# Three Strassen tile pairs per gate chunk, and Strassen tiles in the output projection of a decoder layer, on one core

## The reference, cut to what matters

```
h   = RMSNorm(x)
[u_pool | q | f | i | g | gate_a | gate_b] = h @ W_in       # 2048 x 9216
y_a = W_a( pooled differences of u_pool, mixed in 4 groups )
y_b = W_b( gated linear recurrence of q, f, i, g in 8 heads )
merged = sigmoid(gate_a) * y_a + sigmoid(gate_b) * y_b
x  += merged @ W_out                                        # 2048 x 2048
x  += W_down( silu(conv(u)_gate) * conv(u)_val ),  u = RMSNorm(x) @ W_up
x  += sigmoid(RMSNorm(x) @ W_pg) * (p @ W_ple)
out = RMSNorm(x)
```

## Time and profile before

| What | Value |
|---|---|
| median of three runs | 1432.59 us (1432.58 to 1432.82) |
| the profiled execution | 1433.02 us |
| its span, first to last instruction | 1431.2 us |
| PE busy | 1420.7 us, 99% |
| DVE busy | 1033.4 us, 72% |
| ACT busy | 774.3 us, 54% |
| POOL busy | 171.5 us, 12% |
| share of PE in the chain that ended last | 97% |
| granted TensorE clock, mean | 0.999 |
| transfers | 273.47 MB, 191 GB/s over the span |

### The profile page before, as it was taken

The page is one execution under the profiler, slowest core; times in us unless marked ns, Lnnn a source line. Parts: engine busy times, 40 slices in busy tenths (PEclk is TensorE's granted clock), DMA queues, the critical chain, the costliest instruction groups (busy, mean ns, idle before and its releaser), DMA issues.

```text
span 1431.2 us, 19783 instructions
## 1 busy us (share of the span) xinstructions
PE 1420.7 (99%) x7094; PEld 1207.4 (84%) x7094; DVE 1033.4 (72%) x1284; ACT 774.3 (54%) x937; POOL 171.5 (12%) x115
## 2 busy tenths in 40 slices
PE   9999999999999999999999999999999999999997
PEld 7888888888888888888888888888888888888886
DVE  7676777867577765566777777777777888887755
ACT  7555655545454544455555555555555555555644
POOL 0044144100000000000111101111011110000000
PEclk9999999999999999999999999999999999999999
DMA  9655555455665665466656566565665555566663
GB/s 323 199 176 162 161 170 169 147 189 193 193 204 177 220 236 189 156 206 185 190 176 205 177 191 194 173 204 181 192 193 180 202 197 194 174 197 215 231 200 121
DMA packets 190876, 273.47 MB, mean 191 GB/s; under 512 B 11744, under 2 KB 103136, under 8 KB 190688
## 3 DMA queue, kind: packets, MB, share of 16 engines
q1 hardware_dynamic: 190384, 272.30, 59.4%
q10 hardware_dynamic: 432, 0.37, 0.1%
HBM read 270.53 MB, written 2.10 MB: 190 GB/s over the span
## 4 chain that ended last, share of the span: by engine, by line
PE 97%; DVE 1%; issue 0%; DMA 0%; ACT 0%; SPq 0%; ACTq 0%; POOLq 0%; POOL 0%; DVEq 0%
PE aux L839 11%; PE main L839 11%; PE main L661 10%; PE main L663 10%; PE main L662 10%; PE aux L848 6%; PE main L848 6%; PE main L719 5%; PE main L720 5%; PE main L721 5%; PE aux L719 3%; PE aux L720 3%; PE aux L721 3%; PE aux L662 2%; PE aux L661 2%; PE aux L663 2%
## 5 line engine op out<-in xcount | busy, mean ns | idle before, releaser
L1421 DVE TENSOR_TENSOR w_lo<-raw,w_hi 128x1024 fp32r<-128x1024 f32 (+1 forms) x484 | 596.8, 1244 | 337.8 <-ACT w_hi L1119 337.4
L1119 ACT ACTIVATE w_hi<-raw 128x1024 fp32r<-128x1024 f32 (+1 forms) x484 | 508.6, 1052 | 517.3 <-PE main L663 158.4
L661 PE MATMUL main<-w_hi,xT 128*128 128x512 f32 x510 | 201.4, 395 | 0.5 <-DVE w_lo L1883 0.3
L662 PE MATMUL main<-w_lo,xT 128*128 128x512 f32 x510 | 198.6, 389 | 0.0
L663 PE MATMUL main<-w_hi,xT 128*128 128x512 f32 x510 | 198.5, 389 | 0.0
L839 PE MATMUL aux<-xT,w_hi 128*128 128x512 f32 x704 | 169.8, 391 | 0.0
L839 PE MATMUL main<-xT,w_hi 128*128 128x512 f32 x672 | 163.0, 391 | 0.0
L839 PEld LDWEIGHTS aux<-xT,w_hi 128*128 128x128 f32 x704 | 129.3, 188 | 25.3 <-issue 0.3
L839 PEld LDWEIGHTS main<-xT,w_hi 128*128 128x128 f32 x672 | 123.2, 188 | 23.6
L2007 POOL TENSOR_TENSOR act<-cv 128x512 f32<-128x512 f32 (+1 forms) x22 | 71.9, 3267 | 418.8 <-DVE cv L1645 418.8
L661 PEld LDWEIGHTS main<-w_hi,xT 128*128 128x128 f32 x510 | 95.8, 188 | 20.3 <-DVE xT L1448 1.3
(11 more groups left out here) (305 smaller groups left out, 2115.3 us busy)
## 6 DMA issues: line engine op xcount, KB each, us to landing
raw<-in_w_up SPq DMA_DIRECT2D x336, 256.0 KB
raw<-in_w_in SPq DMA_DIRECT2D x136, 512.0 KB
raw<-in_w_down SPq DMA_DIRECT2D x84, 512.0 KB
raw<-in_w_out SPq DMA_DIRECT2D x32, 512.0 KB
raw<-in_w_ple_gate SPq DMA_DIRECT2D x32, 512.0 KB
raw<-in_w_branch_a SPq DMA_DIRECT2D x16, 512.0 KB
raw<-in_w_branch_b SPq DMA_DIRECT2D x16, 512.0 KB
raw<-in_w_in SPq DMA_DIRECT2D x15, 256.0 KB, 5.9
```

Source lines behind the costliest of these rows:

```text
L661: pe.matmul(acc, th, wh, start=first, stop=False)
L662: pe.matmul(acc, th, wl, start=False, stop=False)
L1119: ac.activation(w_hi[:, u % RING, :, 0:w], raw[:, u % RING, :, 0:w], ACT.Copy).then_inc(hi_full, 1)
L1421: dve.tensor_tensor(w_lo[:, u % RING, :, 0:w], raw[:, u % RING, :, 0:w], w_hi[:, u % RING, :, 0:w].bitcast(F32), ALU.subtract).then_inc(lo ...
```

## The change

- The gate pairs get three Strassen tiles, at i = 1, 3 and 5, in place of two at i = 2 and 4. Their combination moves to two units later, and its first addition to the head of its slot.
- The output projection takes two chunks at once (p = 0: chunks 0 and 1; p = 1: chunks 2 and 3), in an order OUT_ORDER: two row tile pairs of the first chunk, two of the second, then the two chunks in turn for i = 2 to 5, then the last two row tile pairs of the first chunk, then those of the second. Chunk 0 so ends after 14 of the 16 units, chunk 1 after 16. It has Strassen tiles at i = 2 and 4 (p = 0) and i = 3 (p = 1). The combination has eight additions; for p = 0 four in slot 13 and four in slot 14 from the projection's start, for p = 1 two in each of slots 27 to 30.
- The activation sums are numbered as forms: three for the gates, three for the projection (those of i = 2, 4 and 3), then the ten of the down projection; a third place for a form lies in mT_hi and mT_lo. The sums of the gates' forms are made three slots earlier than before, those of the projection's in slots 12 and 9 ahead of it and in its slot 12.
- mT_hi and mT_lo are written at the head of their slot, in place of its end; the transposes x1T go one unit later for three of the four chunks (X1_LAG), with their parts.

The diff, cut to its core:

```diff
+OUT_ORDER = ([(i, a) for a in range(2) for i in range(2)] + [(i, a) for i in range(2, UK - 2) for a in range(2)]
+             + [(i, a) for a in range(2) for i in range(UK - 2, UK)])
+def out_unit(p, i, a=0):
+    return WOUT + 2 * UK * p + OUT_ORDER.index((i, a))
 def out_slot(n):
-    return WOUT + UK * (n + 1)
+    return WOUT + 2 * UK * (n // 2) + 2 * UK - 2 + 2 * (n % 2)
+X1_LAG = (2, 2, 1, 2)
...
-GATES_AT = (2, 4)
+GATES_AT = (1, 3, 5)
+OUT_AT = ((2, 4), (3,))
...
+SUMS_AT = {MIX + 2 * UK - 5 + 3 * f: f for f in range(len(GATES_AT))}
+SUMS_AT.update((WOUT + at, len(GATES_AT) + f) for f, at in enumerate([-12, -9, 12]))
...
-    + [(out_slot(n) + 1, f"x1T{n}") for n in range(NQ)]
+    + [(out_slot(n) + X1_LAG[n], f"x1T{n}") for n in range(NQ)]
...
+OUT_COMBINE_AT = [out_unit(p, OUT_AT[p][-1]) + 5 for p in range(2)]
...
+            def out_seven(u, p, i, a):
+                q = SEVEN[u - a]
+                first, end = i == OUT_AT[p][0], i == OUT_AT[p][-1]
+                pe.wait_ge(lo_full, u + 1)
+                if a == 0:
+                    if first:
+                        if p:
+                            pe.wait_ge(xT_ready, 4 * (NQ + 2))
+                        else:
+                            pe.wait_ge(gated, 4 * NQ)
+                    triple(gate_product(0), *m_block_t(2 * i, 0), *ring_tile(u, 0), start=first, stop=end)
+                    mm = triple(main[:, 0, 0, :], *m_block_t(2 * i + 1, 0), *ring_tile(u, 1), start=False, stop=False)
+                else:
+                    pe.wait_ge(a_sums_ready, FORM[q] + 1)
+                    mm = triple(main[:, 1, 0, :], *act_sum(q, 2), *ring_tile(u, 1), start=False, stop=False)
+                mm.then_inc(units_done, 1)
...
-            for n in range(NQ):
-                for i in range(UK):
-                    if n == 0 and i % 2 == 0:
+            for p in range(2):
+                for i, a in OUT_ORDER:
+                    if p == 0 and a == 0 and i % 2 == 0:
                         pe.wait_ge(mT_ready, i // 2 + 1)
-                    chunk_unit(u, C_WOUT + n, i, UK, mT_hi, mT_lo, 2 * i)
+                    if i == 0:
+                        main_released(C_WOUT + 2 * p + a - 2)
+                    if i in OUT_AT[p]:
+                        out_seven(u, p, i, a)
+                    else:
+                        unit(u, C_WOUT + 2 * p + a, i, UK, mT_hi, mT_lo, 2 * i)
+                    for half in range(2):
+                        if u - 2 - half in SEVEN:
+                            out_weight_sums(u - 2 - half, p, half)
+                    for name in AUX_AT.get(u, ()):
+                        side(name)
...
             def slot(s):                                   # ACT
+                if s - 1 in MT_AT:
+                    merged_hi(MT_AT[s - 1])
...
+                    if s == OUT_COMBINE_AT[p] - 1:
+                        done = 2 * (N_GATES + sum(map(len, OUT_AT[:p + 1])))
+                        ac.wait_ge(w_sums_done, done)
+                        ac.wait_ge(w_sums_ready, done)
+                        ac.activation(w_sums[:, 0, :], gate_product(0), ACT.Copy).then_inc(copied, 1)
...
             def slot(s):                                   # DVE
+                if s - 1 in MT_AT:
+                    merged_lo(MT_AT[s - 1])
+                if s in GATES_COMBINE_AT[1:]:
+                    combine_gates(GATES_COMBINE_AT.index(s), 0)
...
                 for p in range(2):
+                    for part in range(4):
+                        if s == OUT_COMBINE_AT[p] + part // len(OUT_AT[p]):
+                            combine(p, part, out=True)
...
                         if s == at:
                             chunk_done(dve, c)
-                            if norm == 1 and n == 0:
-                                dve.wait_ge(tok_in, 16 * NQ)
-                            if norm == 2:
-                                dve.wait_ge(combined, combines[0])
+                            dve.wait_ge(combined, combines[0])
                             for tb in range(TB):
...
             def join_parts(f):                             # POOL
+                elif f < DOWN_FORMS:
+                    i = OUT_FORMS[f - len(GATES_AT)]
+                    k, hi, lo = 2 * i, mT_hi, mT_lo
+                    pool.wait_ge(mT_ready, i // 2 + 1)
...
                 if f:
                     pool.wait_ge(a_sums_ready, f)
```

More of the change, by code:

```diff
@@ L418, in sums_parts, with form_place, form_parts, form_before @@
             return w_sums_hi, w_sums_lo
+        def form_place(f):
+            return 2 if f == 2 else f % 2
+        def form_parts(f):
+            if f == 2:
+                return [t[:, KD - 4:KD - 2, :].rearrange("p k (h t) -> p (k h) t", t=P) for t in (mT_hi, mT_lo)]
+            return a_sums_hi[:, f % 2], a_sums_lo[:, f % 2]
+        def form_before(f):
+            return max(e for e in range(f) if form_place(e) == form_place(f))
         def down_acc(n, tb):
@@ L550, in _ @@
                         u += 1
[L551 to L553 removed]
+            for p in range(2):
+                for i, a in OUT_ORDER:
+                    rows(u, w_out_v, 2 * i, (2 * p + a) * NCOL)
                     x_tok_piece(u)
@@ L1275, in sums_hi, with merged_hi @@
                                   ACT.Copy).then_inc(w_sums_hi_ready, 1)
+            def merged_hi(n):
+                ac.wait_ge(m_turned, n + 1)
+                ac.activation(mT_hi[:, 4 * n:4 * n + 4, :], m_blocks(), ACT.Copy).then_inc(mT_hi_ready, 1)
             def slot(s):
+                if s - 1 in MT_AT:
+                    merged_hi(MT_AT[s - 1])
                 if s < UK - LEAD:
@@ L1726, in sum_gates, with combine @@
                     dve.tensor_tensor((sig_a, sig_b)[k][:, tb, :], main[:, k, tb, :], t[2 * tb + k], ALU.add).then_inc(gate_sums, 1)
-            def combine(p, part):
+            def combine(p, part, out=False):
                 c0, c1 = cols(2 * p), cols(2 * p + 1)
-                p5, p6, p7 = (product(p, k) for k in range(1, 4))
+                p5, p6, p7 = (gate_product(k) if out else product(p, k) for k in range(1, 4))
                 t = [w_sums[:, k, :] for k in range(4)]
@@ L1739, in combine @@
                 if part == 0:
-                    dve.wait_ge(copied, NQ - 1 + p + 1)
+                    if out and p == 0:
+                        dve.wait_ge(tok_in, 16 * NQ)
+                    dve.wait_ge(copied, NQ - 1 + p + 1 + (0 if out else 2))
                     add(x_tok[:, 0, c0], t[0], x_tok[:, 0, c0])
@@ L2007, in product @@
                 pool.tensor_tensor(act[:, 0:nf, :], cv[:, 0:nf, :], cv[:, nf:2 * nf, :], ALU.mult).then_inc(prod_u, 1)
-            for f in range(2):
-                join_parts(f, 0)
+            for f in range(DOWN_FORMS):
+                join_parts(f)
             root(1)
@@ L2014, in _ @@
                 product(1, 2, it)
-            for f, u in enumerate(ACT_SUMS[2:], 2):
-                join_parts(f, u)
+            for f in range(DOWN_FORMS, N_FORMS):
+                join_parts(f)
             root(2)
```

82 lines of the change are left out of this document (53 added, 29 removed).

## The result

The changed kernel takes 1435.14 us (median of 13 executions, 1434.04 to 1436.58); the kernel before took 1432.58 beside it (13 executions, 1432.06 to 1432.86). The ratio is 1.0019 [1.0012, 1.0026]: 2.6 us slower, where 0.3 us faster was forecast, and 0.14 us above the range. The profiled execution took 1435.16 us, with a span of 1433.4; the span before was 1431.2.

A forecast was written before the change was run, and what follows sets the result against it. PE, busy 1420.7 of 1431.2 us, was taken as the bound, with DVE having little room in the gate pairs. -4.08 - 0.2 + 1.2 + 2.74 = -0.34 gave 1432.3 us from the median, range 1429.0 to 1435.0.

The forecast's parts named there:

- a failure outside all rivals: Anywhere in the kernel: a wait on weight transfers, of which the prediction saw none, would fall outside forecast and rivals.
- Removed matmuls, -4.08: Gate pairs and projection: six more Strassen tiles remove 18 matmuls of 0.2267 us from PE's path, saving 4.08 us.
- The gap at x1T3, -0.2: Start of the up projection: x1T3 transposes, one unit later, no longer wait for the last chunk's additions, saving 0.2 us.
- At W+31 the x1T2 transposes and UP's first matmuls now need chunk 2's additions ... nothing: Projection's end: those additions come 5.1 us after the preceding unit's start, against 5.44 us of PE work, costing nothing.
- The gate pairs, +1.2: Gate chunk pairs: 0.17 us of PE wait in each of three, plus 0.7 in pair 2 from POOL's join; bounds 0 to 4.
- 11.2 (11.3): Gate pairs: DVE finishes mT_lo 11.2 us after the pair's first unit, PE needs it at 11.3, so in time.
- The switch, +2.74: Between projection chunk pairs: PE waits 2.66 us plus 0.08 restart for chunk 0's additions, queued behind eight combinations; bounds 0, 3.5.
- The granted clock does not suffer: At the switch: idle PE keeps clock 1.00, as at the kernel's end from 1423.2 to 1427.9 us; no added cost.
- The sum, -0.34: Whole kernel: saved matmuls and x1T3 gap against gate and switch waits, 0.34 us faster; 1432.3 us from the median.
- (a): Projection's switch: DVE's additions come in time, so no wait; 1429.5 us, or 1428.3 without gate waits; chance 0.24.
- (c): Strassen products: the change saves less than it says, for instance by gaps between products; about 1434 us; chance 0.03.
- (b): Gate pairs: DVE becomes the bound, each pair waits 1.4 us, 4.2 in all; 1436.5 us; chance 0.11.

The follow-up runs named there:

- run 2: Changed kernel with DVE's copy of rB moved ahead of the weight split in its slot, nothing else changed: 1434.33 us, ratio 1.0011.
- run 9: Changed kernel with rB's copy ahead of the split, POOL's join held, chunk 3's additions ahead of x1T2's low parts; switch unchanged: 1433.22 us, ratio 1.0002.
- run 10: As run 9, plus eleven matmuls on PE with unused results in the wait at the switch: 1432.04 us, ratio 0.9997.
- Edit 6: Changed kernel with chunk 3's additions ahead of x1T2's low parts in DVE's slot UP+0: 1434.74 us, ratio 1.0016.
- run 8: Run 7 plus chunk 3's additions ahead of x1T2's low parts, and gate pairs' first product waiting for two gated halves, not four: 1429.03 us, ratio 0.9976.
- run 3: Changed kernel with POOL's join for projection tile i=2 held until gate pair 2's products are done: 1434.61 us, ratio 1.0012.
- Run 7: Changed kernel with chunk 0's additions before the last four combinations, third joint sum later, rB's copy ahead of its split, POOL's join held: 1429.60 us, ratio 0.9977.
- run 5: Changed kernel with chunk 0's own additions ahead of the last four combinations, third joint sum at W+17 instead of W+12: 1431.62 us, ratio 0.9997.
- run 1: Changed kernel with one Strassen tile (i=2) instead of two in the projection's first chunk pair: 1432.76 us, ratio 1.0001.
- run 4: Changed kernel with two Strassen tiles per gate pair (i=2 and 4) as before, projection as in the change: 1434.53 us, ratio 1.0011.
- run 11: As run 8, but two Strassen tiles per gate pair (i=2 and 4) and POOL's join not held: 1430.29 us, ratio 0.9984.

## Why the prediction was wrong

All that it named as signs of being right came: 18 fewer matmuls, 2.66 us of idle PE at the switch, a 2.31 us DVE instruction beside the join, no gap before x1T3. So did the one that it called a failure outside all rivals, a wait that goes back to a weight transfer. Two steps failed: a term put at nothing at the start of the up projection, and the price of the switch's wait. By the medians they are worth 0.8 (the rB wait, run 2) and 1.2 us (the clock, runs 9 and 10). Edit n is that of experiment n.

- **Removed matmuls, -4.08: right.** 18 fewer, and no gaps between products other than those listed above.
- **The gap at x1T3, -0.2: right. The sentence behind it is the first step that failed:** "At W+31 the x1T2 transposes and UP's first matmuls now need chunk 2's additions ... nothing". The count went from T(30) to those additions and stopped. It left out what the moved transposes bring along: x1T2's four low parts on DVE, 1.66 us, which now stand ahead of chunk 3's additions, of the split of UP+4, and so of two transfers and the rB copy. Price 2.05 us in the profile, predicted at nothing. Nor did it look for what had no slack there: rB's copy, with PE right behind it. Edit 6 took away the rstd wait (0.25); edit 2 took away the rB wait. That the 1.66 us cause the rB wait too rests on the chain of starts in the profile: in edit 6, which changes the order of those instructions and not their sum, a part of that wait stayed. No run moved the low parts out of that slot.
- **The gate pairs, +1.2: the mechanism right, the size 1.6.** Pairs 1 and 3 took 0.32 and 0.33 where 0.17 stood: the `gated` wait was 0.11 + 0.08 as worked out, and mT_lo, "11.2 (11.3)", came late by 0.05 and another restart of 0.08. Run 8 shows that the two are one queue: what is gained at the first is lost at the second. Pair 2 took 0.97 where 0.87 stood, 0.65 of it the collision (run 3); the forecast put most of that at unit 8, where 0.11 came, and the rest, 0.52, came at unit 12. POOL's join and DVE's low part took 2.20 and 2.31 beside each other, against 1.22 for the low part alone in run 3. By the rule of the Trainium skill cited ahead (page "SBUF — State Buffer", section "Who interferes with whom") the two exclude each other; the trace agrees, and DVE lost 1.09 us, what the rows gave (1.1), not a whole join of 1.30.
- **The switch, +2.74: right as a gap (2.66 + 0.11), wrong in its price, the second step that failed.** "The granted clock does not suffer" was read from the last microseconds of one execution and carried over to another place. There the clock stayed at 1.00 for 4.7 us with PE idle; at the switch it fell behind a wait of 2.66 us, in seven of run 9's eleven executions. Runs 9 and 10 put 1.2 us on the median.
- **The sum, -0.34: the profile has +2.15.** The difference of 2.5 us is the up projection (2.05) and the gates (0.4). The clock's 1.5 us do not come on top in the median, too, most likely because with the clock fallen PE reaches the up projection later and waits less for rB (0.50 in run 6, with a transfer as slow as the one behind the 1.80). The executions say the same: with a mean clock of 0.997 the median is 1435.06 in the changed kernel and 1434.68 in run 2, so edit 2 brings 0.4; the other executions, four and three, have medians of 1435.56 and 1433.33, so it brings 2.2, as far as so few tell. That fits why edit 2 alone moved the median by 0.8 and not by 1.9. Run 7, with the switch's wait and the rB wait gone, has no execution at 0.997 and gave the whole.
- **The 1.80 is one execution's.** In the five profiles without a fall in which PE waits for rB, the wait is the time from the issue of UP+9's transfer to ACT's start, less 3.0 us: 4.82, 4.51, 3.77, 3.60 and 3.54 give 1.80, 1.50, 0.74, 0.56 and 0.51 (the changed kernel, runs 3, 5, 1 and 4). So the later issue makes the wait possible and the transfer decides its length: 0.5 us where it is fast. Why it takes 3.5 us in one execution and 4.8 in another stays open.
- **Rivals.** (a) and (c) did not come: the switch was there and the saving whole. (b), DVE as the bound in the gates, had the right sign in the wrong place: the gates lost 1.6, not 4.2. The slower side came from two mechanisms that no rival held.

## What to carry to other kernels

When a step is moved to a later slot, follow every instruction it issues on every engine, and at each engine read the slack of what now stands behind it from the trace before, by start times and not by the view of waits alone: rB's copy had none, and 1.75 us came. Put what releases the busiest engine ahead of work that only combines results; here run 8, which reorders work, holds one join back and releases one product earlier, turned 2.6 us slower into 3.6 us faster (0.9976 [0.9967, 0.9986] against the kernel before). A wait on PE of a few microseconds is to be priced with the clock behind it, and a difference between one profile and a median is to be looked for in the spread of the executions.

## What the hardware showed that was not expected

Of the six profiles that have the 2.66 us wait at the switch, one shows a granted clock of 0.50 for 3 us behind it and five show 1.00, though the work around it is the same; in run 9 seven of eleven executions are in the slower group. The share differs from run to run: a mean clock of 0.997 stands in eight of eleven executions of runs 2 and 6, in four of run 3 and in two of run 4, and 0.998 does not rule a fall out (one of run 9's seven has it). Runs 1 and 5, without the wait at the switch, have one and two such executions, 2 to 3 us above their medians, and no profile shows where; runs 7, 8, 10 and 11 have none. What decides it is not shown. Eleven useless matmuls made run 10 1.2 us faster than run 9.
